# A two-layer decoder step: conditioning chunks moved around the seams between sub-layers, and the mixer's output scaled ahead of a wait

## The reference: what is computed

```python
m = (jax.nn.silu(c) @ cond_w + cond_b).reshape(c.shape[0], N_COND, 1, D_MODEL)   # N_COND = 9

def pre(i, h):
    return rmsnorm(h, norm_pre[i]) * (1.0 + m[:, 3 * i + 1]) + m[:, 3 * i]

def post(i, h, y, rw):
    return h + rw * m[:, 3 * i + 2] * rmsnorm(y, norm_post[i])

x = post(0, x, swiglu(pre(0, x), ffn_w_in[0], ffn_w_out[0]), MACARON_W)
o, ... = mixer(pre(1, x), mix_w_in, mix_w_out, ...)
x = post(1, x, o, 1.0)
x = post(2, x, swiglu(pre(2, x), ffn_w_in[1], ffn_w_out[1]), MACARON_W)
```

## Time and profile before

| what | value |
|---|---|
| time, 3 runs | median 1523.11 us (1519.5 to 1530.31) |
| profiled execution | 1520.16 us, of which the span of the program is 1518.6 us |
| granted TensorE clock, mean | 0.961 |
| PE busy | 1392.4 us, 92% of the span |
| PE weight loads (beside the matmuls) | 1301.6 us, 86% |
| DVE busy | 822.9 us, 54% |
| ACT busy | 589.5 us, 39% |
| DMA | 335.16 MB, mean 221 GB/s |

### The profile page before, as it was taken

One profiled execution on the slowest core, in us unless ns is written; L12 is line 12 of the kernel. 1 busy time (PEld: TensorE's weight loads), 2 busy tenths in 40 slices (PEclk: granted clock), 3 DMA queues, 4 the chain that ended last, 5 costly groups with the idle time before them and its releaser, 6 DMA issues.

```text
span 1518.6 us, 36144 instructions
## 1 busy us (share of the span) xinstructions
PE 1392.4 (92%) x13844; PEld 1301.6 (86%) x13844; DVE 822.9 (54%) x1221; ACT 589.5 (39%) x949; POOL 56.5 (4%) x130
## 2 busy tenths in 40 slices
PE   5899999989886899999979999998997778999996
PEld 4899999789764889999969999987995577999996
DVE  2544544657972564554454455355789336455544
ACT  2423333523533543334453333354253345333344
POOL 3000000100110000000000000010002100000000
PEclk9899999999988999999989999999998979999998
DMA  9797597699757795555658858859994769765453
GB/s 313 244 279 220 158 303 219 189 295 292 243 198 239 238 319 160 163 149 150 181 161 278 256 160 253 261 171 282 273 301 163 254 179 322 209 165 166 142 164 113
DMA packets 432268, 335.16 MB, mean 221 GB/s; under 512 B 16087, under 2 KB 356343, under 8 KB 432128
## 3 DMA queue, kind: packets, MB, share of 16 engines
q1 hardware_dynamic: 429556, 327.52, 70.4%
q0 software_dynamic: 2272, 5.61, 1.1%
q10 hardware_dynamic: 300, 0.13, 0.0%
HBM read 328.41 MB, written 4.78 MB: 219 GB/s over the span
## 4 chain that ended last, share of the span: by engine, by line
PE 76%; DVE 7%; DMA 4%; SPq 4%; ACT 3%; issue 3%; DVEq 2%; ACTq 0%
PE PS L554 19%; PE PS L555 19%; PE PS L556 19%; PE PS L578 3%; PE PS L599 2%; PE PS L600 2%; PE PS L601 2%; PE PS L784 2%; SPq L460 2%; SPq L439 1%; PE PS L723 1%; PE PS L830 1%; PE PS L933 1%; DMA direct<-in_cache_sb_v 1%; DMA raw<-in_mix_w_in 1%
## 5 line engine op out<-in xcount | busy, mean ns | idle before, releaser
L1527 DVE TENSOR_TENSOR w_lo<-raw,w_hi 128x1024 fp32r<-128x1024 f32 (+1 forms) x371 | 396.1, 1106 | 530.7 <-ACT w_hi L1181 530.7
L1181 ACT ACTIVATE w_hi<-raw 128x1024 fp32r<-128x1024 f32 (+1 forms) x371 | 339.8, 960 | 726.1 <-PE PS L556 624.9
L554 PE MATMUL PS<-a_hi,w_hi 128*128 128x288 f32 x1664 | 497.9, 299 | 0.1
L555 PE MATMUL PS<-a_lo,w_hi 128*128 128x288 f32 x1664 | 490.9, 295 | 0.0
L556 PE MATMUL PS<-a_hi,w_lo 128*128 128x288 f32 x1664 | 489.3, 294 | 0.0
L554 PEld LDWEIGHTS PS<-a_hi,w_hi 128*128 128x128 f32 x1664 | 312.0, 188 | 8.2 <-issue 7.5
L556 PEld LDWEIGHTS PS<-a_hi,w_lo 128*128 128x128 f32 x1664 | 313.4, 188 | 0.0
L555 PEld LDWEIGHTS PS<-a_lo,w_hi 128*128 128x128 f32 x1664 | 312.4, 188 | 0.2
L554 PE MATMUL PS<-h_hi,w_hi 128*128 128x288 f32 x704 | 209.8, 298 | 0.0
L555 PE MATMUL PS<-h_lo,w_hi 128*128 128x288 f32 x704 | 209.1, 297 | 0.0
L556 PE MATMUL PS<-h_hi,w_lo 128*128 128x288 f32 x704 | 208.5, 296 | 0.0
(11 more groups left out here) (302 smaller groups left out, 1235.9 us busy)
## 6 DMA issues: line engine op xcount, KB each, us to landing
raw<-in_ffn_w_in SPq DMA_DIRECT2D x180, 512.0 KB, 4.8
direct<-in_cond_w SPq DMA_DIRECT2D x320, 256.0 KB, 4.9
direct<-in_cache_sb_k SPq DMA_DIRECT2D x128, 256.0 KB, 4.0
direct<-in_cache_sb_v SPq DMA_DIRECT2D x128, 256.0 KB, 3.8
raw<-in_ffn_w_out SPq DMA_DIRECT2D x64, 384.0 KB, 3.7
raw<-in_mix_w_in SPq DMA_DIRECT2D x48, 512.0 KB, 6.9
raw<-in_ffn_w_out SPq DMA_DIRECT2D x64, 320.0 KB, 4.1
raw<-in_mix_w_out SPq DMA_DIRECT2D x16, 512.0 KB, 6.0
```

The lines of the kernel that those rows point to most:

```text
L554: pe.matmul(out, whi, hi, start=begins and i == 0, stop=False)
L555: pe.matmul(out, whi, lo, start=False, stop=False)
L1181: act.activation(w_hi[:, s, at_:at_ + n], raw[:, s, at_:at_ + n], ACT.Copy)\
L1527: tt(w_lo[:, s, at_:at_ + n], raw[:, s, at_:at_ + n], w_hi[:, s, at_:at_ + n], ALU.subtract).then_inc(lo_done.sem, 1)
```

## The change

There are three edits. On SP the loads of chunks 0 to 3 for seam 1 stand between the output projection's weight steps 1 and 2, where they stood behind the second FFN's first two steps. On PE the count of chunks ahead of the squares of seam 0 goes from three to four: chunk 8 changes sides. On DVE six of the eight gating instructions of the mixer's output stand ahead of the wait for its last two blocks. No instruction is added or taken away.

```diff
@@ sync: behind the mixer @@
                 for s in range(2):
                     mix(l, mix_w_out, POS_MO, s, s, s * 256)
+                cond_seam(l, 0, 0, 4)
                 for s in range(2):
                     mix(l, mix_w_out, POS_MO, 2 + s, s, (2 + s) * 256)
                 for s in range(2):
                     ffn_in(l, 1, s, s)
-                cond_seam(l, 0, 0, 8)
+                cond_seam(l, 0, 4, 8)
                 ffn(l, 1)
@@ tensor @@
                 ffn(l, 0, (0, DP_C[1]))
-                filled_seam(l, 0, 1, DP_C[2], 5, 8)
+                filled_seam(l, 0, 1, DP_C[2], 5, 9)
@@ vector @@
                 tt(yacc[:, :, :], yacc[:, :, :], ysq[:, 0:2, :], ALU.add).then_inc(y_summed.sem, 1)
-                seam_post(l, 1, YB_MO + 2 + N_MO, 0, (l, POS_IN[1]), 0)
+                gate_prompt(1, 0, KB - 2)
+                seam_post(l, 1, YB_MO + 2 + N_MO, KB - 2, (l, POS_IN[1]), 0)
                 pre(l, 2, (l, POS_IN[1]))
```

## The result

| kernel | median us | lowest to highest | runs |
|---|---|---|---|
| before | 1520.43 | 1513.26 to 1530.31 | 17 |
| changed | 1528.03 | 1524.12 to 1534.62 | 17 |

The changed kernel takes 1.0046 of the time of the kernel before, 95% interval 1.0032 to 1.0059: a little slower, half of what would count as a difference in the chances given ahead. The forecast was 1527. Part of that nearness is luck: the sum was +5.2 us, put on a base that lay between 1520.16 and 1523.11, while the difference of the medians is 7.6. The changed kernel's profiled execution took 1526.18 us, with a span of 1524.7, which is 6.1 us more than the span before.

The account below looks back on a forecast made before the run. PE held 76% of the chain of waits, so edits matter at the seams. Terms +12.0 (seam 0), -6.0 (loads), -0.8 (gates) gave +5.2 us; predicted 1527 us, range 1517 to 1535, chance 0.90 within 1%.

Parts of the forecast that it names:

- the sum: Whole kernel: seam 0 +12.0, seam 1 loads -6.0 and gates -0.8, together +5.2 us.
- Seam 0, the wait: Seam 0: PE stands 5.2 us before chunk 8 for DVE's copy; `rstd` 3.8 us late at the full clock.
- Seam 0, the clock: Seam 0: PE's work behind the hole runs at 1.2 GHz, losing 1.6 to 3.0 us; 2.2 taken.
- PE's slack of 1.4 us: Mixer start: PE's first product follows `a_lo` by 1.4 us; nothing subtracted, since the chain leaves by DVE and SP.
- Seam 1, the loads: Seam 1: sooner loads of chunks 0 to 3 bring `rstd` forward, -1.7 us in layer 0, -4.3 in layer 1.
- the gates' part: Seam 1: six sooner gates on DVE gain 0.4 us a layer, -0.8 in all.
- Cover enough: Seam 1: chunks 4 to 6 land before the first product; the third near 536, run before 539.6.
- 3 us to spare: Output projection: step 2 lands at 499.5 or 501.0, ACT wants it at 504.29; costed at nothing.
- (first): Seam 0: the clock stays up; +0.8 us, 1521 to 1524; chance 10%.
- (second): Mixer: it absorbs seam 0's delay; with none arriving -6.8 us, 1513 to 1516; chance 8%.
- (third): Seam 0: the copy does not hold chunk 8, a miscount; -6.8 us, 1513 to 1516; chance 4%.
- (fourth): Output projection: step 2 starves behind the four chunks, 7.5 us late a layer; about 1540 to 1543; chance 8%.

Follow-up runs that it names:

- the kernel with the filled hole: The whole change plus twenty matmuls that nobody reads ahead of chunk 8 in seam 0, against the kernel before: ratio 0.9995.

## Why the forecast was right, point by point

- **Seam 0, the wait.** It stood at 5.2 us and was 5.30, released by the copy as counted. The copy that PE waits for took 0.30 rather than 0.24, since two that follow each other overlap. What it costs the norm was 3.8 and measured 3.9 with the clock kept up.
- **Seam 0, the clock.** It stood at 2.2, taken between 1.6 and 3.0, and is 2.0. Together +6.0 a layer forecast, +5.91 and +5.94 measured. The fall to 1.2 GHz was read from two other waits, one for DVE and one for ACT, and it held. That 2.2 came within 0.2 is partly luck: the middle of a range was taken, and by the last section a term of the clock can differ by 2 us between two runs of the same seam.
- **PE's slack of 1.4 us.** In the changed kernel PE's first product comes 4.47 us behind `rstd` in seam 0, where it was 5.76 and 6.36. So PE starts the mixer 4.6 and 4.1 us late and not 5.9, yet the mixers are shorter by 0.7 and 0.2 only, which is within their scatter. To subtract nothing was nearly right; the delay went on through DVE and SP.
- **Seam 1, the loads.** -1.7 and -4.3 forecast, with the gates -2.1 and -4.7, and -2.1 and -4.7 measured. Loads alone against both: the gates' part is 0.39, forecast 0.4. Against rows of the kernel before, the loads alone took 1.69 off layer 0 and 4.29 off layer 1.
- **"Cover enough" for chunks 4 to 6 was wrong.** The third was to land near 536, ten us behind the first `rstd`. In the changed kernel SP starts on them at 532.44 and PE gets the third only at 544.93, 13.5 us behind. The start was as costed, 1 us behind `rstd`. What was too small is the time from a DMA's issue to its landing, which the forecast took from bytes at 387 GB/s alone. The first landed 2.9 us after its issue. The third chunk's last went out at 538.4 and landed 6.4 us later, and from 534 to 542 us the queues moved 310 to 345 GB/s. SP's issue by itself (16 DMAs in 9.15 us, so 2.3 us a chunk) was quicker than the 2.7 us a chunk of the forecast. The first product so comes 5.36 and 5.19 us behind `rstd` rather than 4.46, a cost of 0.9 and 0.7. Of that 0.4 and 0.2 are left at the end of the FFN, for the stretch from the first product to the end of the second FFN is 0.5 us shorter (220.10 against 220.63). Why it is shorter was not tried.

```profile
532.44 9.15 SPq L439 DMA_DIRECT2D direct<-in_cond_w  x16
```

- **"3 us to spare" ahead of step 2 was too much.** The landing had been costed at 13.5 to 15 us after the slot of chunk 3 came free, from the transfer of four chunks (10.8 us). In layer 0 of the changed kernel the slot came free at 490.1, and the step's two loads went out at 500.2 and 500.8 and landed 8.2 and 9.5 us later, at 508.4 and 510.3, 18 to 20 us after the slot and about when ACT needed them; in the changed kernel the second half of step 2 waits 0.37 us in layer 1. It cost PE nothing, so the sum was not hurt.
- **The end.** The last seam's squares took 7.12 us rather than 5.87, both at the lower clock for a part, +1.3 us behind the last `rstd`. The change does not touch it. With the mixers and the FFN rows it makes the +6.1 of the span out of +5.1. The medians differ by 7.6; the interval is 4.9 to 9.0, and the sum of +5.2 lies at its lower end.

The rivals: the clock did not stay up (first); the mixer absorbed at most 0.2 to 0.7 of 5.9 us (second); the copy held chunk 8 (third); the output projection did not starve, though it stood at the point from which it would (fourth), and the one time that it was made to, a step earlier in the queue, the price was about 7 us a layer by the medians; the forecast had 7.5 for step 2.

What stays open is why the rest of the span moved by 1 us, why the kernel with the filled hole gained more than its seams show, and whether the copy moved sooner costs 0.1 us in seam 0 (9.29 and 9.31 against 9.20 and 9.19).

## What to carry to other kernels

Before an instruction is moved ahead on an engine that executes in order, count out by which increment its wait is met, and look where the instruction that gives it stands: a buffer's copy that cost nothing behind a wait becomes the wait. Price the hole twice, once as time and once as the slower clock of all that follows on PE. And cost a load that is to be ready soon from a measured time between issue and landing on a queue as full as it will be, as well as from its bytes.

## What the runs showed of the hardware that was not expected

- Matmuls that nobody reads can be worth their place: with 29 of them a layer in the mixer's waits the ratio went from 0.9947 and 0.9951 to 0.9919. The six mixers with them took 229.13, 230.90, 234.01, 232.36, 234.31 and 231.31 us, against 234.62, 234.54, 234.08 and 230.54 without, which alone would prove little. The stretch from the last value chunk to the projection's first product shows it: 8.74 to 11.43 us in all six, against 12.23 or 12.24 in all four. They only help where PE would wait anyway: 22 of them at the layer's turn, begun at the lower clock, took 6.78 us and put the first product 3.1 us later.
- The same waits don't always lower the clock: behind waits of 1.5 to 1.6 us for loads the squares of seam 1 of layer 0 took 4.15 us in the kernel before and 6.15 with chunk 8 alone. So a term of the clock has a spread of 2 us a seam that no edit explains.
- Where a layer's loop turns, PE and DVE stand for about 2.9 us with no wait that the profile shows (`issue`), and the clock is low behind it even where the squares ahead ran at the full one (1.00 from 774 to 778 us, 0.76 from 779 to 786): 44 filler rows took 6.78 us there, against 40 in 4.73 in the filled hole.
